# The block inverses of a gated delta rule: the two lower levels made in quadrants on the diagonal of the array

## Chip, cores and metric

The kernel runs on one core of one Trainium2 chip. The metric is the device time of one execution in microseconds (us). The time before is the median of three runs.

## What is computed

The reference is one transformer block over 1024 tokens: a projection, a gated delta rule with 8 heads, a sparse attention with 8 heads, and a gated merge of the two. The part that matters here is the delta rule. Per head and chunk of tokens a lower triangular system is solved:

```python
a_mat = where(strict, einsum('bhnid,bhnjd->bhnij', kb, k) * gamma, 0.0)
sol = triangular_solve(a_mat + eye, rhs, left_side=True, lower=True)
```

The kernel works with chunks of 128 tokens (the recurrence gives the same result for any chunk), so a head has `NT` = 8 systems of 128x128, and it makes the inverse of each rather than solving with it.

## The kernel before

The kernel has three phases: a front phase, the delta phase (`phase_delta`, line 1105) and attention with the merge. In the delta phase all engines walk through one list of slots, written out by hand. A head starts every 24 slots, and `u` is the slot counted from the head's start. In each slot TensorE first does a quarter of a projection (`project`, line 1805: six 16-bit matmuls of 128x512, by the helper `three`, lines 94 to 96), then the recurrence of up to two older heads (`recur`, lines 1937 to 1958, fp32 matmuls of 128x128), and in some slots a group of small fp32 matmuls of a head. The order on every engine is the order of the program; semaphores make one engine wait for another.

The inverse is built in levels. VectorE, ScalarE and GpSimd first make the inverses of the 16x16 diagonal blocks (`substitute` on GpSimd, `expand` on VectorE at u = 31). Then two neighbouring blocks of size b are joined, for b = 16, 32 and 64. The corner of the joined inverse is minus (lower block's inverse) x (corner of the system) x (upper block's inverse), so each level is two groups of matmuls with a step of another engine after each:

- b = 16: `middle16` (u 34, line 1886) multiplies the system `a_t` with `flip16`; VectorE masks the result out of PSUM into `x16` (u 35, line 1742); `outer16` (u 36, line 1892) multiplies `x16` with columns of `t2`; VectorE subtracts the result from `t2` (line 1726) and turns two 32x32 blocks per tile into `flip32` (line 1644).
- b = 32: `middle32` (u 38, line 1898); ScalarE copies PSUM to `x32` (line 1500); `outer32` (u 40, line 1904); VectorE subtracts two corners (line 1717) and turns three blocks into `flip64`.
- b = 64: `middle64` (u 42, line 1910), a copy (line 1496), `outer64` (u 44, line 1916), a subtraction (line 1709).

The groups of b = 16 and 32 use the full 128x128 array with 64 moving columns, since all blocks of a tile are handled in one matmul and mixed terms are zeroed by masks. The groups of b = 64 work on 64 rows and 64 columns of the array. Each group has 8 matmuls, one per tile. An fp32 matmul is two records in the trace, each with a weight load of its own. `middle` groups write PSUM bank 2, `outer` groups bank 3. `x16` and `x32` are the same memory, so VectorE zeroes the odd blocks again for each head (line 1737, u 46).

Of the kernel before, what the change touches and what calls it, by code (L numbers as in the profile page):

```python
# [25 lines left out]
P = 128  # L26
# [33 lines left out]
def constant_table():  # L60

    t = np.zeros((P, K_ALL), np.float32)
    i = np.arange(P)
    row, col = i[:, None], i[None, :]
    t[:, K_ID:K_ID + P] = row == col
    t[:, K_FLIP:K_FLIP + P] = row + col == P - 1
    t[:, K_UPTO:K_UPTO + P] = row <= col
    t[:, K_AFTER:K_AFTER + P] = row > col
    t[:, K_ONES:K_ONES + P] = 1.0
    t[:, K_CAUSAL:K_CAUSAL + P] = np.where(col > row, BELOW, 0)  # L70
    t[:, K_BLOCK:K_BLOCK + P] = row // 16 == col // 16

    short = np.arange(64)[None, :]
    t[:, K_PAIR:K_PAIR + 64] = row // 16 == 2 * (short // 16) + 1
    t[:, K_UNIT:K_UNIT + 16] = row % 16 == np.arange(16)[None, :]
    return t
# [1028 lines left out]
def phase_delta(nc, g, block):  # L1105

    with ExitStack() as ctx:
# [9 lines left out]
        prep = g.shared[:, 0:3 * T].rearrange("p (n t) -> p n t", t=T)  # L1117
        gam, x16 = (prep[:, n].rearrange("p (i n) -> p i n", n=P) for n in (0, 2))
        a_t = [part.rearrange("p (i n) -> p i n", n=P) for part in (prep[:, 1], g.arena[:, 10 * T:11 * T])]
# [9 lines left out]
        flip = lb[:, 0:NT * 32].rearrange("p (t two i) -> p t two i", two=2, i=32)  # L1129
        flip16 = lb[:, T // 2:T].rearrange("p (i n) -> p i n", n=64)  # L1130
        flip32, flip64 = (g.arena[:, (22 + n) * T // 2:(23 + n) * T // 2].rearrange("p (i n) -> p i n", n=64) for n in range(2))
        x32 = x16
        sq_junk, o_junk = sb("sq_junk", [P, 4, P], BF16), sb("o_junk", [P, P], BF16)
# [25 lines left out]
        at = lambda k, i: g.ps[:, k * BANK + i * P:k * BANK + (i + 1) * P]  # L1159
        half_at = lambda k, i: g.ps[:, k * BANK + i * 64:k * BANK + (i + 1) * 64]  # L1160
        win = g.w_in[0].rearrange("(k p) n -> p k n", p=P)
        wo = g.w_o_gdn[0].rearrange("(k p) n -> p k n", p=P)
# [208 lines left out]
        def _(act):  # L1371
# [108 lines left out]
            for slot in range(END):  # L1480
# [10 lines left out]
                for h in heads(slot):  # L1491
                    u = slot - SLOTS * h
                    if u == 42:
                        act.wait_ge(xm, 3 * h + 3)
                        act.wait_ge(tx, 3 * h + 2)
                        nc.scalar.copy(x32[64:128, :, 0:64], short(2)[64:128]).then_inc(x_ok, 1)
# [46 lines left out]
        def _(dve):  # L1543
            nc.vector.memset(raw[:, :, 0:PAD], 0.0).then_inc(pad, 1)
            nc.vector.memset(x16, 0.0).then_inc(pad, 1)
            nc.vector.memset(g.arena[:, 11 * T:12 * T], 0.0).then_inc(pad, 1)
            nc.vector.tensor_scalar(unseen, unseen, CLOSED, None, ALU.mult).then_inc(consts, 1)
# [76 lines left out]
            def expand(h):  # L1624
# [5 lines left out]
                for odd in range(2):  # L1630
# [5 lines left out]
                dve.wait_ge(turned, 2 * h + 2)  # L1636
                shape = [P, NT, 4, BASE]
                nc.vector.tensor_tensor(flip16.rearrange("p t (c i) -> p t c i", i=BASE),
                                        flip.rearrange("p t two i -> p (t two) i")[:, :, 0:BASE].unsqueeze(2).broadcast_to(shape),
                                        g.const[:, K_BLOCK:K_BLOCK + P].rearrange("p (c two i) -> p c two i", two=2, i=BASE)[:, :, 0].unsqueeze(1).broadcast_to(shape),  # L1640
                                        ALU.mult).then_inc(flip_ok, 1)

# [26 lines left out]
            for slot in range(END):  # L1669
# [7 lines left out]
                for h in heads(slot):  # L1677
# [34 lines left out]
                    if u == 40:  # L1712
                        dve.wait_ge(tx, 3 * h + 2)
                        for b in (0, 2):
                            odd, even = slice(32 * b + 32, 32 * b + 64), slice(32 * b, 32 * b + 32)
                            cols = slice(16 * b, 16 * b + 32)
                            nc.vector.tensor_tensor(t2[even, h % 3, :, odd], t2[even, h % 3, :, odd], short(3)[even, :, cols], ALU.subtract).then_inc(up, 1)
                        dve.wait_ge(up, 3 * h + 3)
# [5 lines left out]
                    if u == 36:  # L1724
                        dve.wait_ge(tx, 3 * h + 1)
                        nc.vector.tensor_tensor(blocks(t2[:, h % 3], 16, 1), blocks(t2[:, h % 3], 16, 1), short(3).rearrange("p i (c w) -> p i c w", w=16),
                                                ALU.subtract).then_inc(up, 1)
                        dve.wait_ge(up, 3 * h + 1)
# [3 lines left out]
                        flip_blocks(flip32, h, 0, 0, 0, 0)  # L1732
                        flip_blocks(flip32, h, 2, 2, 2, 1).then_inc(flip_ok, 1)
                    if u == 46:
                        dve.wait_ge(tx, 3 * h + 3)
                        dve.wait_ge(x_ok, 2 * h + 2)
                        nc.vector.memset(blocks(x16, 16, 1), 0.0).then_inc(pad, 1)
                    if u == 35:
                        dve.wait_ge(xm, 3 * h + 1)
                        dve.wait_ge(pad, 3 + h)  # L1740
                        shape = [P, NT, 4, 16]
# [60 lines left out]
        def _(pe):  # L1802
# [78 lines left out]
            def middle16(h):  # L1881
# [31 lines left out]
            def outer64(h):  # L1913
                pe.wait_ge(x_ok, 2 * h + 2)
                for i in range(NT):
                    last = mm(half_at(3, i)[0:64], x32[64:128, i, 0:64], t2[64:128, h % 3, i, 64:128], start=True, stop=True)
                last.then_inc(tx, 1)
# [711 lines left out]
```

## Time and profile before

| | us |
|---|---|
| median of 3 runs | 1448.59 (1444.6 to 1449.78) |
| the profiled execution | 1444.3 |
| its span, first to last instruction | 1442.2 |
| TensorE busy | 1402.8 (97%) |
| VectorE busy | 930.5 (65%) |
| ScalarE busy | 714.9 (50%) |
| GpSimd busy | 600.9 (42%) |
| mean granted TensorE clock | 0.995 |

TensorE's "busy" is the union of its matmuls' durations, and these overlap: a 128x512 matmul lasts 0.38 us and the next one starts 0.22 us after it. So costs on TensorE are read from the distance between starts in the timeline. PE is TensorE's matmuls, PEld its weight loads, DVE VectorE, ACT ScalarE, POOL GpSimd.

### The profile page before, as it was taken

Reading aid. Unit: us, or ns where it says so; the run is one execution under the profiler, and the core shown is the slowest. Engines: PE = TensorE matmul, PEld = TensorE weight load, DVE = VectorE, ACT = ScalarE, POOL = GpSimd, SP = SyncE. Lnnn points to the kernel's source line nnn. Section 1 sums busy time; section 2 is a strip of 40 time slices with the busy share of each in tenths; the row PEclk is TensorE's granted clock in tenths of the full one; section 3 lists DMA queues with packets and bytes.
Section 4 is the critical chain, followed back from the end, with each engine's and each line's share of the span. In section 5 each row is a group of like instructions: output and inputs, shape, how many; then the busy total and the mean of one; then the engine's idle time right before and its main releaser. Section 6 shows DMA issues by size and latency. Waiting matters only on the chain.

```text
span 1442.2 us, 26031 instructions
## 1 busy us (share of the span) xinstructions
PE 1402.8 (97%) x9792; PEld 872.8 (61%) x9792; DVE 930.5 (65%) x1946; ACT 714.9 (50%) x1513; POOL 600.9 (42%) x717
## 2 busy tenths in 40 slices
PE   6899999999999899999999999999999999999997
PEld 6546984444444567667667677655445888844444
DVE  3969777777335567678777775545724777737344
ACT  4848777785434544554555554333123777711111
POOL 0083677778652542541531521003022877764000
PEclk9999999999999999999999999999999999999999
DMA  9410343333224222231222322336663000075132
GB/s 373 122 37 2 105 118 118 117 106 117 88 80 130 73 61 71 63 90 45 76 61 62 89 61 74 103 103 222 198 217 141 28 19 31 16 266 175 36 107 88
DMA packets 137637, 147.43 MB, mean 102 GB/s; under 512 B 16706, under 2 KB 109738, under 8 KB 135852
## 3 DMA queue, kind: packets, MB, share of 16 engines
q1 hardware_dynamic: 136668, 141.31, 31.0%
q10 hardware_dynamic: 720, 4.46, 0.8%
q8 instruction: 77, 1.26, 0.4%
q14 instruction: 44, 0.36, 0.1%
q0 software_dynamic: 128, 0.03, 0.0%
HBM read 114.40 MB, written 31.15 MB: 101 GB/s over the span
## 4 chain that ended last, share of the span: by engine, by line
PE 61%; DVE 3%; ACT 2%; issue 1%; POOL 1%; DMA 0%; SPq 0%; DVEq 0%; ACTq 0%; POOLq 0%
PE ps L94 15%; PE ps L96 15%; PE ps L95 15%; PE ps L2368 2%; DVE g_yq L1562 1%; PE ps L1937 1%; PE ps L1892 1%; PE ps L1840 1%; PE ps L1904 1%; PE ps L1898 1%; DVE g_o L1697 1%; PE ps L1878 1%; PE ps L1958 1%; PE ps L1886 1%; PE ps L1942 1%
## 5 line engine op out<-in xcount | busy, mean ns | idle before, releaser
L94 PE MATMUL ps<-g_h_hi,g_piece_hi 128*128 128x512 f16 x544 | 206.7, 380 | 1.6 <-PEq L2579 1.6
L95 PE MATMUL ps<-g_h_lo,g_piece_hi 128*128 128x512 f16 x544 | 206.4, 379 | 0.0
L96 PE MATMUL ps<-g_h_hi,g_piece_lo 128*128 128x512 f16 x544 | 206.4, 379 | 0.0
L1328 POOL TENSOR_TENSOR g_shared<-g_shared 128x120 f32<-128x120 f32 (+14 forms) x120 | 56.5, 471 | 207.5 <-DMA g_shared<-diagonal_blocks 196.9
L946 DVE TENSOR_SCALAR_CACHE_REDUCE a_ada<-a_ada,a_s_all 128x896 bf16<-128x896 f32 (+1 forms) x124 | 113.1, 968 | 1.0
L94 PE MATMUL ps<-g_o,g_h_hi 128*128 128x128 f16 (+2 forms) x424 | 101.4, 266 | 1.7 <-DVE l_b L2489 1.6
L96 PE MATMUL ps<-g_o,g_h_lo 128*128 128x128 f16 (+2 forms) x424 | 101.4, 266 | 0.0
L95 PE MATMUL ps<-g_o,g_h_hi 128*128 128x128 f16 (+2 forms) x424 | 101.4, 266 | 0.0
L96 PEld LDWEIGHTS ps<-g_h_hi,g_piece_lo 128*128 128x128 bf16 x544 | 53.3, 98 | 64.4 <-issue 0.5
L1562 DVE SCALAR_TENSOR_TENSOR g_yq<-e_raw,g_taps,g_yq 128x1024 f32<-128x1024 f32 x60 | 86.5, 1442 | 8.8 <-ACT g_yq L1392 7.1
L94 PEld LDWEIGHTS ps<-g_h_hi,g_piece_hi 128*128 128x128 f16 x544 | 54.8, 101 | 53.4 <-issue 2.3
L95 PEld LDWEIGHTS ps<-g_h_lo,g_piece_hi 128*128 128x128 f16 x544 | 53.4, 98 | 51.2 <-issue 0.3
L2531 POOL TENSOR_SCALAR g_o<-g_o,l_share 128x128 f32<-128x128 f32 (+3 forms) x64 | 47.9, 749 | 80.0 <-DVE l_share L2474 79.6
L1553 DVE TENSOR_TENSOR g_piece_lo<-g_piece,g_piece_hi 128x1024 bf16<-128x1024 f32 x40 | 53.2, 1330 | 21.6 <-ACT g_piece_hi L1475 21.6
L1424 ACT ACTIVATE g_shared<-ps,e_s_neg 128x128 f32<-128x128 f32 x56 | 20.6, 367 | 93.5 <-PE ps L1942 93.2
L302 POOL TENSOR_TENSOR a_work<-a_w,a_work 128x512 bf16<-128x512 f32 x48 | 56.6, 1194 | 15.3 <-ACT a_work L683 15.3
L302 POOL TENSOR_TENSOR a_parts<-a_w,a_parts 128x512 bf16<-128x512 f32 x48 | 54.9, 1157 | 13.3 <-ACT a_parts L683 13.3
L2414 ACT ACTIVATE g_o<-g_o,l_top 128x128 f32<-128x128 f32 (+3 forms) x64 | 49.7, 776 | 20.7 <-DVE l_top L2467 18.7
L1330 POOL TENSOR_TENSOR g_shared<-g_shared 128x120 f32<-128x120 f32 (+14 forms) x120 | 54.1, 451 | 9.4
L700 ACT ACTIVATE a_ada<-a_ada,a_s_all 128x1024 bf16<-128x1024 f32 (+1 forms) x62 | 57.3, 927 | 0.5 <-DVEq L968 0.5
L1475 ACT CAST g_piece_hi<-g_piece 128x1024 f16<-128x1024 f32 x40 | 41.7, 1042 | 29.0 <-DMA g_piece<-in_w_o_gdn 28.0
L2423 ACT CAST g_o<-ps 128x128 f16<-128x128 f32 (+3 forms) x64 | 40.7, 637 | 26.5 <-PE ps L2368 24.9
(431 smaller groups left out, 4127.9 us busy)
## 6 DMA issues: line engine op xcount, KB each, us to landing
a_w<-in_w_in SPq DMA_DIRECT2D x17, 1024.0 KB, 5.7
g_piece<-in_w_in SPq DMA_DIRECT2D x34, 512.0 KB, 3.9
channel_gates<-a_ada SPq DMA_DIRECT2D x48, 256.0 KB, 2.2
g_shared<-diagonal_blocks SPq DMA_DIRECT2D x32, 256.0 KB
a_ada<-in_w_ada ACTq DMA_DIRECT2D x4, 1024.0 KB, 9.4
a_x<-in_x SPq DMA_DIRECT2D x8, 512.0 KB, 8.8
delta_gate<-a_ada SPq DMA_DIRECT2D x16, 256.0 KB, 2.5
g_shared<-sums_by_head SPq DMA_DIRECT2D x8, 512.0 KB, 3.9
```

Source lines behind the costliest of these rows:

```text
L94: pe.matmul(out, a_hi, b_hi, start=first, stop=False)
L95: pe.matmul(out, a_hi, b_lo, start=False, stop=False)
L96: return pe.matmul(out, a_lo, b_hi, start=False, stop=last)
L302: nc.gpsimd.tensor_tensor(op_lo[v % 2][:, x], of, op_hi[v % 2][:, x], ALU.subtract).then_inc(w_ready, 1)
L700: nc.scalar.activation(mask[:, g.first[i]:g.first[i + 1]], score[:, g.first[i]:g.first[i + 1]], ACT.Sign, bias=trial[:, 4 + e:5 + e], accu ...
L946: mark(("count", e), nc.vector.tensor_scalar(spent_of(i), rows_of(i), trial[:, e:e + 1], offset[:, e:e + 1], ALU.is_ge, ALU.add, accum_out ...
L1328: nc.gpsimd.tensor_tensor(part, table[:, j, :, j + 1:BASE], tc[:, :, j:j + 1].broadcast_to([P, NT, left]), ALU.mult).then_inc(sub, 1)
L1330: last = nc.gpsimd.tensor_tensor(tc[:, :, j + 1:BASE], tc[:, :, j + 1:BASE], part, ALU.subtract)
L1553: nc.vector.tensor_tensor(w_lo[:, m % 3], w32[:], w_hi[:, m % 3], ALU.subtract).then_inc(w_ready, 1)
L1562: nc.vector.scalar_tensor_tensor(out=y, in0=raw[:, m % 2, PAD - 3 + j:PAD - 3 + j + T], scalar=g.taps[:, tap:tap + 1], in1=y, op0=ALU.mult ...
L2414: nc.scalar.activation(p(n), p(n), ACT.Exp, scale=-1.0, bias=top[:, n % 4:n % 4 + 1], accum_out=total[:, n % 4:n % 4 + 1]).then_inc(exp_ok, 1)
L2531: nc.gpsimd.tensor_scalar(p(m), p(m), share[:, m % 4:m % 4 + 1], 1.0, ALU.mult, ALU.mult).then_inc(shared, 1)
```

## The change

The matmuls of b = 16 and b = 32 are split. For b = 16 the two 64x64 quadrants on the diagonal of the array are used, one matmul for each: 64 rows, 64 columns, 32 moving columns. For b = 32 a matmul uses 32 rows and 32 columns with 32 moving columns, in row groups 0 and 64 (`middle32`) or 32 and 96 (`outer32`). So each of the four groups has 16 matmuls in place of 8, alternating between the upper and the lower half. The upper half writes PSUM bank 2, the lower half bank 3, and `middle` and `outer` have separate halves of a bank. `flip16`, `flip32`, `x16` shrink to 32 columns per tile; `x32` and `x64` get memory of their own, so the zeroing of line 1737 goes. VectorE's mask and subtraction of b = 16 and ScalarE's copy of b = 32 become two instructions each, one per half. The b = 64 groups are unchanged but for where `x64` lies.

```diff
             def middle16(h):
...
                 for i in range(NT):
-                    last = mm(half_at(2, i), a_t[h % 2][:, i], flip16[:, i], start=True, stop=True)
+                    for half in range(HALVES):
+                        rows = quadrant(half)
+                        last = mm(edge(half, 0, i)[rows], a_t[h % 2][rows, i, rows], flip16[rows, i], start=True, stop=True)
             def outer16(h):
...
-                    last = mm(half_at(3, i), x16[:, i], columns(t2[:, h % 3, i], 16, 1), start=True, stop=True)
+                    for half in range(HALVES):
+                        rows = quadrant(half)
+                        last = mm(edge(half, 1, i)[rows], x16[rows, i], columns(t2[rows, h % 3, i, rows], 16, 1), start=True, stop=True)
             def middle32(h):
...
-                    last = mm(half_at(2, i), a_t[h % 2][:, i], flip32[:, i], start=True, stop=True)
+                    for half in range(HALVES):
+                        last = mm(edge(half, 0, i)[odd(half)], a_t[h % 2][even(half), i, odd(half)], flip32[even(half), i], start=True, stop=True)
             def outer32(h):
...
-                    last = mm(half_at(3, i), x32[:, i], columns(t2[:, h % 3, i], 32, 1), start=True, stop=True)
+                    for half in range(HALVES):
+                        last = mm(edge(half, 1, i)[even(half)], x32[odd(half), i], t2[odd(half), h % 3, i, odd(half)], start=True, stop=True)
...
+        edge = lambda half, part, i: g.ps[:, (2 + half) * BANK + part * 256 + i * 32:(2 + half) * BANK + part * 256 + (i + 1) * 32]
+        edges = lambda half, part, rows: g.ps[rows, (2 + half) * BANK + part * 256:(2 + half) * BANK + (part + 1) * 256].rearrange("p (i n) -> p i n", n=32)
+        quadrant = lambda half: slice(64 * half, 64 * half + 64)
...
                     if u == 38:
...
-                        nc.scalar.copy(blocks(x32, 32, 0), short(2).rearrange("p i (c w) -> p i c w", w=32)).then_inc(x_ok, 1)
+                        nc.scalar.copy(x32[odd(0)], edges(0, 0, odd(0)))
+                        nc.scalar.copy(x32[odd(1)], edges(1, 0, odd(1))).then_inc(x_ok, 1)
...
                     if u == 36:
...
-                        nc.vector.tensor_tensor(blocks(t2[:, h % 3], 16, 1), blocks(t2[:, h % 3], 16, 1), short(3).rearrange("p i (c w) -> p i c w", w=16),
-                                                ALU.subtract).then_inc(up, 1)
+                        for half in range(HALVES):
+                            rows = quadrant(half)
+                            corners = blocks(t2[rows, h % 3, :, rows], 16, 1)
+                            last = nc.vector.tensor_tensor(corners, corners, edges(half, 1, rows).rearrange("p i (c w) -> p i c w", w=16), ALU.subtract)
+                        last.then_inc(up, 1)
...
-                    if u == 46:
...
-                        nc.vector.memset(blocks(x16, 16, 1), 0.0).then_inc(pad, 1)
                     if u == 35:
...
-                        nc.vector.tensor_tensor(blocks(x16, 16, 0), short(2).rearrange("p i (c w) -> p i c w", w=16),
-                                                g.const[:, K_PAIR:K_PAIR + 64].rearrange("p (c w) -> p c w", w=16).unsqueeze(1).broadcast_to(shape),
-                                                ALU.mult).then_inc(x16_ok, 1)
+                        for half in range(HALVES):
+                            rows = quadrant(half)
+                            last = nc.vector.tensor_tensor(blocks(x16[rows], 16, 0), edges(half, 0, rows).rearrange("p i (c w) -> p i c w", w=16),
+                                                           lower[rows].unsqueeze(1).broadcast_to([64, NT, 2, 16]), ALU.mult)
+                        last.then_inc(x16_ok, 1)
```

## Rows read from the trace of the kernel before

**Rows 1.** The page, 40 slices: PE busy tenths, granted clock tenths

```profile
PE   6899999999999899999999999999999999999997
...
PEclk9999999999999999999999999999999999999999
```

**Rows 2.** Stretches of the delta phase: us, busy us (instructions) by engine, clock

```profile
480.00:530.00 50.00, 45.32 (x276) 30.34 (x275) 31.22 (x59) 19.15 (x38) 19.57 (x35) 0.93 0.22 61
530.00:880.00 350.00, 346.69 (x2315) 240.02 (x2315) 263.56 (x572) 188.53 (x472) 129.38 (x218) 1.00 0.24 68
```

**Rows 3.** Waits of TensorE from 530 to 880 us: total, times, longest

```profile
PE ps L1937 <- DVE g_o L1666: 2.6, 2, 1.4
```

**Rows 4.** Line 1892: durations in ns, forms, how many records

```profile
L1892 PE MATMUL ps<-g_arena,g_shared x128: 222/275/422, 499.4 to 891.7; 128*128 128x64 f32 x128
```

**Rows 5.** Timeline of TensorE, head 1: start us, length us, what, xcount

```profile
547.54 1.90 PE L1886 MATMUL ps<-g_shared,g_arena 128*128 128x64 f32 x16
549.27 0.38 PE L94 MATMUL ps<-g_h_hi,g_piece_hi 128*128 128x512 f16 x1
...
552.31 1.90 PE L1892 MATMUL ps<-g_arena,g_shared 128*128 128x64 f32 x16
...
558.69 1.90 PE L1898 MATMUL ps<-g_arena 128*128 128x64 f32 x16
...
563.46 1.90 PE L1904 MATMUL ps<-g_arena,g_shared 128*128 128x64 f32 x16
```

**Rows 6.** The same timeline at the groups on a quadrant of 64x64

```profile
568.23 1.04 PE L1851 MATMUL ps<-g_const,g_shared 128*128 128x128 f32 x8
569.20 1.14 PE L1910 MATMUL ps<-g_arena 64*64 64x64 f32 x16
570.27 0.39 PE L94 MATMUL ps<-g_h_hi,g_piece_hi 128*128 128x512 f16 x1
```

**Rows 7.** Front phase: six matmuls on two row groups of 64 rows, and their forms

```profile
103.57 0.82 PE L480 MATMUL ps<-a_ada 64*128 64x512 f16 x6 [0.24 <-DVE a_ada L1051]
```

**Rows 8.** Forms and durations (ns) of those six, from 103.5 to 104.1 us

```profile
L480 PE MATMUL ps<-a_ada x6: 323/354/387, 103.6 to 104.0; 64*128 64x512 f16 x3, 64*128 64x384 f16 x3
```

**Rows 9.** Front phase timeline: small fp32 matmuls with 24 rows and 24 moving columns

```profile
90.54 0.42 PE L454 MATMUL ps<-g_const,a_ada 24*128 24x24 f32 x4
```

**Rows 10.** Attention phase timeline: first and last of 27 matmuls in a row

```profile
1151.94 0.22 PE L94 MATMUL ps<-g_o,g_h_hi 128*128 128x128 f16 x1
...
1153.39 0.22 PE L96 MATMUL ps<-g_arena 128*128 128x128 f16 x1
```

**Rows 11.** Other engines by line and form: total us, mean ns, idle before

```profile
L1638 DVE TENSOR_TENSOR g_shared<-g_shared,g_const 128x512 f32<-128x512 f32 x8 | 9.8, 1219 | 0.0
L1717 DVE TENSOR_TENSOR g_arena<-g_arena,ps 32x256 f32<-32x256 f32 x16 | 6.6, 414 | 12.3 <-PE ps L1904 12.0
L1742 DVE TENSOR_TENSOR g_shared<-ps,g_const 128x512 f32<-128x512 f32 x8 | 5.4, 678 | 1.8 <-PE ps L1886 1.8
L2221 DVE TENSOR_TENSOR g_arena<-g_arena 128x256 f32<-128x256 f32 x2 | 0.8, 425 | 0.1
L1737 DVE MEMSET g_shared<- 128x512 f32 x8 | 3.9, 485 | 0.4
L1500 ACT COPY g_shared<-ps 128x512 f32<-128x512 f32 x8 | 4.7, 586 | 38.7 <-PE ps L1898 38.7
L2423 ACT CAST g_o<-ps 128x256 f16<-128x256 f32 x8 | 3.0, 370 | 1.4 <-PE ps L2368 1.3
```

**Rows 12.** Timeline of VectorE and ScalarE between the groups of head 1

```profile
550.59 0.68 DVE L1742 TENSOR_TENSOR g_shared<-ps,g_const 128x512 f32<-128x512 f32 x1
554.97 0.88 DVE L1644 STREAM_TRANSPOSE g_arena<-g_arena 32x256 f32<-32x256 f32 x2
560.63 0.59 ACT L1500 COPY g_shared<-ps 128x512 f32<-128x512 f32 x1 [4.20 <-PE ps L1898]
```

More of the change, by code:

```diff
@@ L73, in constant_table @@
     short = np.arange(64)[None, :]
-    t[:, K_PAIR:K_PAIR + 64] = row // 16 == 2 * (short // 16) + 1
+    t[:, K_PAIR:K_PAIR + 64] = row // 16 % 4 == 2 * (short // 16 % 2) + 1 - short // 32
     t[:, K_UNIT:K_UNIT + 16] = row % 16 == np.arange(16)[None, :]
@@ L1117, in phase_delta @@
         prep = g.shared[:, 0:3 * T].rearrange("p (n t) -> p n t", t=T)
[L1118 removed]
+        gam = prep[:, 0].rearrange("p (i n) -> p i n", n=P)
+        x16, x32 = (prep[:, 2, c0:c0 + NT * n].rearrange("p (i n) -> p i n", n=n) for c0, n in ((0, 64), (NT * 64, 32)))
         a_t = [part.rearrange("p (i n) -> p i n", n=P) for part in (prep[:, 1], g.arena[:, 10 * T:11 * T])]
@@ L1129, in phase_delta @@
         flip = lb[:, 0:NT * 32].rearrange("p (t two i) -> p t two i", two=2, i=32)
-        flip16 = lb[:, T // 2:T].rearrange("p (i n) -> p i n", n=64)
-        flip32, flip64 = (g.arena[:, (22 + n) * T // 2:(23 + n) * T // 2].rearrange("p (i n) -> p i n", n=64) for n in range(2))
-        x32 = x16
+        flip16 = lb[:, T // 2:3 * T // 4].rearrange("p (i n) -> p i n", n=32)
+        flip32 = g.arena[:, 11 * T:11 * T + NT * 32].rearrange("p (i n) -> p i n", n=32)
+        flip64, x64 = (g.arena[rows, 23 * T // 2:12 * T].rearrange("p (i n) -> p i n", n=64) for rows in (slice(0, 64), slice(64, P)))
+        lower, upper = (g.const[:, c0:c0 + 32].rearrange("p (c w) -> p c w", w=BASE) for c0 in (K_PAIR, K_PAIR + 32))
         sq_junk, o_junk = sb("sq_junk", [P, 4, P], BF16), sb("o_junk", [P, P], BF16)
@@ L1160, in phase_delta @@
         half_at = lambda k, i: g.ps[:, k * BANK + i * 64:k * BANK + (i + 1) * 64]
+        edge = lambda half, part, i: g.ps[:, (2 + half) * BANK + part * 256 + i * 32:(2 + half) * BANK + part * 256 + (i + 1) * 32]
+        edges = lambda half, part, rows: g.ps[rows, (2 + half) * BANK + part * 256:(2 + half) * BANK + (part + 1) * 256].rearrange("p (i n) -> p i n", n=32)
+        quadrant = lambda half: slice(64 * half, 64 * half + 64)
+        even, odd = (lambda half, e=e: slice(64 * half + 32 * e, 64 * half + 32 * e + 32) for e in range(2))
         win = g.w_in[0].rearrange("(k p) n -> p k n", p=P)
@@ L1495, in _ @@
                         act.wait_ge(tx, 3 * h + 2)
-                        nc.scalar.copy(x32[64:128, :, 0:64], short(2)[64:128]).then_inc(x_ok, 1)
+                        nc.scalar.copy(x64, short(2)[64:128]).then_inc(x_ok, 1)
                     if u == 38:
@@ L1636, in expand @@
                 dve.wait_ge(turned, 2 * h + 2)
-                shape = [P, NT, 4, BASE]
+                shape = [P, NT, 2, BASE]
                 nc.vector.tensor_tensor(flip16.rearrange("p t (c i) -> p t c i", i=BASE),
                                         flip.rearrange("p t two i -> p (t two) i")[:, :, 0:BASE].unsqueeze(2).broadcast_to(shape),
-                                        g.const[:, K_BLOCK:K_BLOCK + P].rearrange("p (c two i) -> p c two i", two=2, i=BASE)[:, :, 0].unsqueeze(1).broadcast_to(shape),
-                                        ALU.mult).then_inc(flip_ok, 1)
+                                        upper.unsqueeze(1).broadcast_to(shape), ALU.mult).then_inc(flip_ok, 1)
             def flip_blocks(out, h, rows, cols, to_rows, to_cols):
@@ L1713, in _ @@
                         dve.wait_ge(tx, 3 * h + 2)
[L1714 to L1717, printed above, removed]
+                        for half in range(HALVES):
+                            corner = t2[even(half), h % 3, :, odd(half)]
+                            nc.vector.tensor_tensor(corner, corner, edges(half, 1, even(half)), ALU.subtract).then_inc(up, 1)
                         dve.wait_ge(up, 3 * h + 3)
@@ L1903, in outer32 @@
                 for i in range(NT):
-                    last = mm(half_at(3, i), x32[:, i], columns(t2[:, h % 3, i], 32, 1), start=True, stop=True)
+                    for half in range(HALVES):
+                        last = mm(edge(half, 1, i)[even(half)], x32[odd(half), i], t2[odd(half), h % 3, i, odd(half)], start=True, stop=True)
                 last.then_inc(tx, 1)
@@ L1915, in outer64 @@
                 for i in range(NT):
-                    last = mm(half_at(3, i)[0:64], x32[64:128, i, 0:64], t2[64:128, h % 3, i, 64:128], start=True, stop=True)
+                    last = mm(half_at(3, i)[0:64], x64[:, i], t2[64:128, h % 3, i, 64:128], start=True, stop=True)
                 last.then_inc(tx, 1)
```

9 lines of the change are left out of this document (3 added, 6 removed).

## The prediction, made before the changed kernel was run

> **What bounds the kernel now.** I read first the page's slices. TensorE stands at nine tenths or more in nearly every slice and its clock is granted in full [rows 1], so it is never slowed by idling and every later price is read at the 2.4 GHz level. "Busy" on TensorE can hide slack, so next come the stretches and the waits. From 530 to 880 us, six of the eight heads, TensorE is busy 346.7 of 350.0 us; VectorE is second with 263.6, that is 75% [rows 2]. The largest wait of TensorE in that stretch is 2.6 us in all [rows 3], against 350. So in the delta phase TensorE's instruction stream is the bound: a microsecond taken off it should shorten the kernel by nearly one, until something that TensorE waits for is late. The first head, 480 to 530, is looser (45.3 of 50) [rows 2].
>
> **How the groups are paid now.** A group is paid by the distance from its first start to the next group's first start. `middle16` starts at 547.54 and the following matmul at 549.27: 1.73 us [rows 5]. Line 1892 has 128 records, and 8 heads x 8 matmuls x 2 records are 128 [rows 4]; lines 1886, 1898 and 1904 have the same shape and the same length of 1.90 us [rows 5]. The step between two records is (1.90 - 0.275)/15 = 108 ns, with 0.275 the duration of one [rows 4, 5]. That is as much as a step of line 1851, with 128 moving columns where this has 64: 0.97/8 is at most 121 ns [rows 6]. So moving columns don't set it; the weights' 128 columns do. Cutting the weights' columns is therefore the lever, and the change cuts them to 64 and to 32, at twice the number of records (32 per group).
>
> **The price of a 64x64 record** stands in the trace: line 1910 starts at 569.20 and the next matmul at 570.27, 1.07 us for 16 [rows 6]. It has 64 moving columns where the new ones have 32, so this is an upper bound for one quadrant. Entering costs something as well: eight records of line 1851 at (1.04 - 0.275)/7 = 0.109 each are 0.87, but the distance to line 1910 is 0.97 [rows 6], so 0.10 us more. The new groups at b = 16 lie, like the old, between full-array matmuls, so each enters and leaves once: 1.07 + 0.10 = 1.17 us for one quadrant's 16 records.
>
> **The disputed term: do the two quadrants run at the same time?** If yes, a b = 16 group costs about 1.17 (both quadrants lie beside each other). If no, the second quadrant's 16 records come behind the first: (1.14 - 0.22)/15 = 61 ns each, so 1.17 + 16 x 0.061 = 2.15 us, which is above the 1.73 of now. The nearest rows for overlap are six matmuls on two row groups of 64 rows in the front phase: three of 512 and three of 384 columns [rows 8] took 0.82 us in all [rows 7]. One after the other they would need at least 3 x 0.216 + 2 x 0.162 + 0.32 = 1.29 us (0.216 is the step of 512 columns, 0.162 that scaled to 384, 0.32 the last one's duration [rows 8]). So matmuls of different row groups did run beside each other, and each went to another bank, as the two halves do in the change. What these rows don't show is the same for fp32 weights, or for groups of columns. I take overlap.
>
> **b = 16**: 1.73 - 1.17 = 0.56 us saved per group, 16 groups (2 x 8 heads): 9.0 us. From the other side: 1.73 - 2.15, 6.7 us lost.
>
> **b = 32**: weights of 32x32. No row has this form. From 128 to 64 weight columns the step fell from 108 to 61 ns, 0.73 ns a column; 32 columns further down it would be 61 - 24 = 37 ns, and 16 records in a quadrant save another 16 x 0.024 = 0.38 us: 0.79 for a group. The other end is that nothing goes below some 60 ns: the smallest fp32 matmuls in the trace, 24 rows and 24 moving columns, took 0.42 us for four, (0.42 - 0.215)/3 = 68 ns a step [rows 9], though their weights had 128 columns. Then a group costs 1.17 as at b = 16. I take 0.90, nearer the first, since the step fell with the columns in the rows of the same kind: 1.73 - 0.90 = 0.83 us, 16 groups: 13.3 us. Ends with overlap: 9.0 and 15.0; without it: 0.79 + 16 x 0.037 = 1.38, 5.6 saved, or 2.15, 6.7 lost.
>
> The Trainium skill, "TensorEngine Tiling (Array Packing)", section Instruction Overhead, says a matmul carries about 60 cycles of overhead and that one should not tile a dimension that is small already. An estimate from that page: 32 records x 25 ns = 0.8 us, with entering and leaving about 1.05 for b = 32, which would make the sum 2.4 us smaller. No run so far shows records of different quadrants at that density; the sum above doesn't use it.
>
> **VectorE.** Mask and subtraction at b = 16: one instruction of 128x512 at 0.68 us becomes two of 64 rows and 256 elements; 256 elements from PSUM took 0.41 [rows 11], so +0.15 each, twice. `flip16`'s product halves: 1.22 us mean for 512 elements, 0.43 for an addition of 256 in the same memory [rows 11], so -0.6 to -0.8. The zeroing, 0.49, goes [rows 11]. Sum per head -0.8 us, of some 42: a head's period is (891.7 - 1.7 - 499.4)/7 = 56 us [rows 4], and 75% of it is 42. ScalarE's copy of 0.59 becomes two of about 0.37 [rows 11]: +0.15. None of this is on TensorE's stream; it decides only whether TensorE finds its inputs.
>
> **What is late next.** Head 1: the mask ends at 551.27 and `outer16` starts at 552.31, 1.0 us later; the turned blocks are ready at 555.85 for `middle32` at 558.69, 2.8 us; ScalarE's copy ends at 561.22 for `outer32` at 563.46, 2.2 us [rows 5, 12]. Between two groups lie the projections and recurrence of two slots, 552.31 - 549.27 = 3.0 us [rows 5], that stay. With `middle16` shorter the mask can still only start when VectorE is free, so of the 1.0 us about 1.0 - 0.56 - 0.15 = 0.3 is left. So the groups don't yet stall each other, but the four groups lie within 17 us and gain 2.8 us there, and the recurrence behind them waits on VectorE too. VectorE would be at 41 of 53 us per head, 78%. I charge 10% of the gain for such waits: what queues behind a late group is the next projection, so it is paid in full.
>
> **Sum.** 9.0 + 13.3 = 22.3 us; less 10% is 20 us. The profiled execution took 1444.3 us, 2.1 above its span; that would be 1424. It lies 4.3 below the median of the three runs, 1448.59, and since I forecast a median I apply the 20 us there: 1428.5 us. Likeliest case's own range: 13 us (waits eat 30%, b = 32 at 1.17) to 28 us (b = 32 at 0.79, no waits, a few us from VectorE's relief): 1420 to 1436.
>
> **Rivals.**
>
> 1. *The quadrants go one after the other, each at its columns' price.* Then b = 16 loses 6.7 and b = 32 wins 5.6: 1 us slower, 1450. For it: no fp32 row shows overlap, and the two records of one fp32 matmul follow each other on the same quadrant, so the order is AABB and the hardware must look two records ahead. Against: rows 7. Chance 0.10.
>
> 2. *Every record costs some 60 ns, whatever its size and quadrant* (an issue price). 32 records instead of 16: each group 2.15, 32 groups x 0.42 = 13 us slower: 1462. It decides once a record costs on average more than (1.73 - 0.10 - 0.15)/31 = 48 ns, where 0.15 is the distance at leaving, 1.07 less 15 steps of 0.061. For it: no fp32 step in the trace is under 60 ns. Against: 16-bit matmuls of attention go at (1153.39 - 1151.94)/26 = 56 ns [rows 10], which is about what their 128 columns need, and the six of rows 7 came closer together. The Trainium skill, "TensorE: Matmul & The Clock Gate", section Back-to-back issue gap, knows such a price, about 62 ns per matmul when the sequencer decodes in software; an estimate from it is 32 x 62 ns = 2.0 us a group, the same outcome. Chance 0.09.
>
> 3. *Overlap as forecast, but VectorE's order takes the gain back*: the mask and the turned blocks come late, TensorE waits at `outer16` and at line 1937, and only half of the 22 us arrives: 1438. For it: VectorE at 75% with little slack at `outer16`. Against: the stretches between groups, 3.0 us for two slots, are already shorter than any slot pair with a group will be, and TensorE doesn't wait in them. Chance 0.13.
>
> Forecast 0.68. What a measurement of this kernel can tell from no change is about 0.5%, 7 us. Faster by over 0.5%: forecast and most of rival 3, and a little of rival 1 if b = 32 does better: 0.78. Within 0.5%: 0.13. Slower: rival 2: 0.09. The range for 8 in 10 is 1418 to 1446: below, the best of all terms; above, rival 3 and the better half of rival 1.
>
> **What would show it.** The group of `middle16`: 32 records within 1.1 to 1.2 us, start to next start, and single starts of the lower half only a few ns from the upper half's. If the group lasts about 2.1, overlap is wrong; if b = 16 lasts 1.2 and b = 32 the same, the columns' price has a floor. TensorE's waits from 530 to 880 us should grow from 3 us to no more than some 5; if they grow by over 8, rival 3 is right. The period of a head should go from 56 to about 53.5 us. My forecast is wrong if the time is above 1436 or below 1420.

## The result, and the profile after

| | before | after |
|---|---|---|
| median, us | 1448.72 (4 runs) | 1423.54 (1422.03 to 1429.42, 4 runs) |
| ratio, 95% interval | | 0.9838 (0.9806 to 0.9869) |
| span of the profiled execution, us | 1442.2 | 1419.9 |
| TensorE busy, us | 1402.8 | 1375.4 |
| VectorE busy, us | 930.5 | 926.2 |
| waits of TensorE from 480 to 930 us | 7.9 | 11.0 |
| first record of `middle16` to last of `outer64`, starts, us | 490.9 to 912.3 | 491.0 to 888.5 |

The kernel is 25 us faster at the median, 22.3 in the profiled executions. Forecast were 20 us and 1428.5, likeliest 1420 to 1436, range 1418 to 1446.

First the groups of head 1 in the timeline of TensorE in the changed kernel (start us, length us, line, shapes, xcount, idle before), to be set beside rows 5:

```profile
539.46 0.39 PE L1953 MATMUL ps<-g_shared,g_yq 128*128 128x128 f32 x2
539.78 1.12 PE L1893 MATMUL ps<-g_shared,g_arena 64*64 64x32 f32 x32
540.83 0.39 PE L94 MATMUL ps<-g_h_hi,g_piece_hi 128*128 128x512 f16 x1
...
546.36 1.12 PE L1901 MATMUL ps<-g_arena,g_shared 64*64 64x32 f32 x32 [2.32 <-DVE g_shared L1747]
...
553.52 0.38 PE L1948 MATMUL ps<-g_shared,g_yq 128*128 128x128 f32 x2
553.84 0.69 PE L1908 MATMUL ps<-g_arena 32*32 32x32 f32 x32
554.47 0.39 PE L94 MATMUL ps<-g_h_hi,g_piece_hi 128*128 128x512 f16 x1
```

`middle16` (now line 1893) takes 540.83 - 539.78 = 1.05 us with 32 records, where it took 1.73 with 16 [rows 5]. That is the footprint of 16 records of 64x64 on one quadrant [rows 6], so the second quadrant's 16 cost nothing: in the trace a record of one half starts 6 to 7 ns after one of the other, and the next pair mostly 51 to 52 ns later. `middle32` (line 1908) takes 554.47 - 553.84 = 0.63 us. Both are entered 0.10 us late: two records of line 1953 are 0.22 us, and the distance is 539.78 - 539.46 = 0.32. In all eight heads the 32 groups have these lengths within 4 ns, where no wait falls into them.

The waits of TensorE from 480 to 930 us, in the kernel before and then in the changed one (who waits, for whom, total us, times, longest); the line left out of the first is that of rows 3:

```profile
PE ps L1892 <- DVE g_shared L1742: 4.0, 1, 4.0
...
PE ps L1886 <- DVE g_shared L1638: 0.7, 1, 0.7
PE ps L1937 <- DVE g_o L1663: 0.6, 3, 0.2
```

```profile
PE ps L1901 <- DVE g_shared L1747: 5.1, 2, 2.8
PE ps L1948 <- DVE g_o L1672: 3.3, 3, 1.4
PE ps L1948 <- DVE g_o L1669: 1.7, 3, 0.7
PE ps L1893 <- DVE g_shared L1645: 0.9, 1, 0.9
```

The stream became 16 x (1.73 - 1.05 - 0.10) = 9.3 us shorter at b = 16 and 16 x (1.73 - 0.63 - 0.10) = 16.0 at b = 32, 25.3 in all. Against it stand 11.0 - 7.9 = 3.1 us more of waits in the delta phase. The new one is the one with the thinnest slack of rows 5 and 12: `outer16` of head 1 waits 2.3 us for the mask, which lies behind a convolution in VectorE's order. The others are the recurrence. One more wait, which the kernel before doesn't have, comes at 1028 us, behind the heads (view from 930 us on):

```profile
PE ps L2019 <- DVE g_arena L1793: 1.6, 1, 1.6
```

The last term is TensorE's clock. In the kernel before it fell after the 4.0 us wait of the first head. In the changed one it stayed at 1.00 there, in spite of a wait of 2.8 us, and fell after the 2.3 us wait in head 1. First a stretch of the kernel before, then two of the changed one (the number behind the last bracket is the granted clock), and line 1845 with 16 records in head 0 and in head 1 of the changed kernel:

```profile
500.00:510.00 10.00, 10.00 (x51) 8.05 (x51) 6.54 (x30) 4.21 (x5) 0.00 (x0) 0.66 0.02 3
```

```profile
540.00:550.00 10.00, 7.68 (x94) 6.09 (x91) 9.21 (x18) 4.92 (x8) 5.60 (x3) 0.89 0.02 5
550.00:560.00 10.00, 10.00 (x107) 5.81 (x107) 8.23 (x31) 3.81 (x10) 0.00 (x0) 0.94 0.23 56
```

```profile
498.64 2.05 PE L1845 MATMUL ps<-g_yq 128*128 128x128 f32 x16
...
547.41 3.41 PE L1845 MATMUL ps<-g_yq 128*128 128x128 f32 x16
```

In head 1 the 16 records lie mostly at the 1.2 GHz level, in head 0 at 2.4. The lower clock cost about 10 x 0.34 = 3.4 us before and 10 x (0.11 + 0.06) = 1.7 us after, so 1.7 us were given back. With it the books of these two executions close: 25.3 - 3.1 - 1.6 + 1.7 = 22.3 us, and the span became 22.3 shorter. The stretch of the heads (last row of the table) became 23.9 shorter, which is 25.3 - 3.1 + 1.7. Waits and clock differ between executions, though. Two more profiled executions of the changed kernel (the repeats below) have 7.9 and 9.4 us of waits from 480 to 930 us, and 2.9 and 1.2 us at line 2019. So only the 25.3 us of the stream is the same in all; new waits take 2.7 to 4.7 us of it.

VectorE and ScalarE in the changed kernel, by line and form (total us, mean ns, idle before):

```profile
L1645 DVE TENSOR_TENSOR g_shared<-g_shared,g_const 128x256 f32<-128x256 f32 x8 | 11.5, 1436 | 0.0
L1734 DVE TENSOR_TENSOR g_arena<-g_arena,ps 64x256 f32<-64x256 f32 x16 | 6.7, 418 | 6.4 <-PE ps L1901 6.3
L1747 DVE TENSOR_TENSOR g_shared<-ps,g_const 64x256 f32<-64x256 f32 x16 | 6.7, 416 | 1.3 <-PE ps L1893 1.2
L1506 ACT COPY g_shared<-ps 32x256 f32<-32x256 f32 x8 | 2.9, 362 | 21.0 <-PE ps L1908 21.0
```

The halves cost what rows 11 said: 0.42 us each on VectorE, 0.36 on ScalarE. `flip16`'s product (line 1645) has a mean of 1.44 us with half the elements, where it was 1.22 [rows 11], but both means mix two cases. In four heads it took 0.41 us, where the same product took 0.68 in six heads of the kernel before. In the other four it took 2.13 to 2.57 us, and each time an instruction of 128x1024 was running on GpSimd (line 1348 or 1344) and VectorE's product ended 0.3 us after it:

```profile
536.87 0.42 DVE L1645 TENSOR_TENSOR g_shared<-g_shared,g_const 128x256 f32<-128x256 f32 x1
...
641.53 3.21 POOL L1348 TENSOR_TENSOR g_shared<-g_shared,g_const 128x1024 f32<-128x1024 f32 x1
...
642.45 2.56 DVE L1645 TENSOR_TENSOR g_shared<-g_shared,g_const 128x256 f32<-128x256 f32 x1
```

In the kernel before that met two heads, with 2.84 us. So half the elements save 0.27 us, and the product met GpSimd's instruction in two heads more.

### The profile page after: what moved, and what is told of

Its sections match the earlier page's. It is cut to its first block, busy times and chain, and to the rows that moved or that the text cites. A ratio compares the mean times of both kernels' runs of the same rounds, so it can differ in the third digit from the quotient of the medians.

```text
span 1419.9 us, 27055 instructions
## 1 busy us (share of the span) xinstructions
PE 1375.4 (97%) x10296; PEld 840.6 (59%) x10304; DVE 926.2 (65%) x1954; ACT 716.5 (50%) x1521; POOL 596.5 (42%) x717
## 4 chain that ended last, share of the span: by engine, by line
PE 53%; DVE 6%; DMA 3%; issue 2%; ACT 2%; POOL 2%; SPq 1%; DVEq 0%; POOLq 0%; ACTq 0%
PE ps L94 14%; PE ps L96 14%; PE ps L95 13%; DVE g_yq L1569 2%; PE ps L2379 2%; DMA merge_half<-g_shared 1%; DVE g_o L1703 1%; POOL g_shared L1334 1%; PE ps L1948 1%; PE ps L1845 1%; POOL g_shared L1336 1%; PE ps L1969 1%; PE ps L1953 1%; PE ps L1952 1%; PE ps L1968 1%
## 5 line engine op out<-in xcount | busy, mean ns | idle before, releaser
L94 PE MATMUL ps<-g_o,g_h_hi 128*128 128x128 f16 (+2 forms) x424 | 101.4, 266 | 1.7 <-DVE l_b L2500 1.6
L95 PE MATMUL ps<-g_o,g_h_hi 128*128 128x128 f16 (+2 forms) x416 | 98.3, 264 | 0.0
L1560 DVE TENSOR_TENSOR g_piece_lo<-g_piece,g_piece_hi 128x1024 bf16<-128x1024 f32 x40 | 50.0, 1250 | 22.8 <-ACT g_piece_hi L1481 22.8
L302 POOL TENSOR_TENSOR a_parts<-a_w,a_parts 128x512 bf16<-128x512 f32 x48 | 55.0, 1161 | 13.3 <-ACT a_parts L683 13.3
```

Of the source, the lines that this page charges most:

```text
L94: pe.matmul(out, a_hi, b_hi, start=first, stop=False)
L95: pe.matmul(out, a_hi, b_lo, start=False, stop=False)
L302: nc.gpsimd.tensor_tensor(op_lo[v % 2][:, x], of, op_hi[v % 2][:, x], ALU.subtract).then_inc(w_ready, 1)
L1560: nc.vector.tensor_tensor(w_lo[:, m % 3], w32[:], w_hi[:, m % 3], ALU.subtract).then_inc(w_ready, 1)
```

## The experiments

Each kernel below is an edit of the changed kernel. Times are medians; "group" is the distance from a group's first start to the next matmul, without the 0.10 us for entering. The runs came in three sets, each with its own runs of the kernel before: 1449.69 (first four), 1448.4 (next four), 1450.54 us (last three). The ratio and its interval are computed from the single runs of both kernels and are not the quotient of the two medians.

| run | median us | ratio to before (95%) | group b = 16 | group b = 32 |
|---|---|---|---|---|
| only b = 32 | 1435.07 | 0.9888 (0.9838 to 0.9938) | 1.73 | 0.63 |
| halves outermost | 1442.4 | 0.9946 (0.9923 to 0.997) | 1.77 | 1.03 |
| same rows | 1422.89 | 0.9802 (0.975 to 0.9854) | 1.05 | 0.63 |
| same columns | 1424.73 | 0.9812 (0.9756 to 0.9868) | 1.05 | 0.63 |
| same tile | 1446.05 | 0.9986 (0.9959 to 1.0012) | 1.98 | 1.13 |
| one bank | 1425.56 | 0.9866 (0.9822 to 0.9909) | 1.05 | 0.63 |
| four tiles | 1422.26 | 0.9844 (0.9789 to 0.99) | 0.66 | 0.63 |
| changed kernel again | 1425.5 | 0.9854 (0.9807 to 0.99) | 1.05 | 0.63 |
| runs of four | 1431.91 | 0.9876 (0.9856 to 0.9897) | 1.36 | 0.83 |
| four tiles, one set of columns | 1418.03 | 0.9777 (0.9748 to 0.9805) | 0.66 | 0.63 |
| changed kernel, third time | 1425.24 | 0.9834 (0.9813 to 0.9854) | 1.05 | 0.63 |

**One part alone.** The b = 16 groups, mask and subtraction go back to full width:

```diff
-                    for half in range(HALVES):
-                        rows = quadrant(half)
-                        last = mm(edge(half, 0, i)[rows], a_t[h % 2][rows, i, rows], flip16[rows, i], start=True, stop=True)
+                    last = mm(half_at(2, i), a_t[h % 2][:, i], flip16[:, i], start=True, stop=True)
```

> Only the b = 32 groups stay in 32x32 tiles; the b = 16 groups go back to the full array with 64 moving columns (x32 keeps memory of its own, so the zeroing stays away). In the changed kernel a b = 16 group took 1.05 us from its start to the next group's start and 0.09 more to enter, a b = 32 group 0.63 and 0.09, against 1.73 before. Theory (TensorE's stream is the bound and each group pays its own footprint): 16 groups x (1.73 - 1.15) = 9.4 us are given back, less a part of the some 3 us that waits took: 1431 to 1433. Rival (the gain is in VectorE's relief, -0.8 us per head, and in waits, not in the footprints): nearly the whole gain of 25 us stays, about 1425.

Measured 1435.1, in its profile the groups at 1.73 and 0.63. Against the changed kernel's 1423.5 to 1425.5 that gives back 10 to 12 us where the footprints say 9.4, and lies 2 us above the 1431 to 1433 expected. In the profiled executions the stretch from the first record of `middle16` to the last of `outer64` is 404.3 us where the changed kernel's is 397.5, so 6.8 us are given back, with 3.0 us less of waits. So the gain follows the footprints of the groups, and the larger share, some 14.6 us against before in the same set, is b = 32's.

**The halves one after the other.**

```diff
-                for i in range(NT):
-                    for half in range(HALVES):
+                for half in range(HALVES):
+                    for i in range(NT):
```

> The changed kernel with the two loops of the four groups exchanged: first the eight tiles of the upper half (16 records), then the eight of the lower half. The same matmuls, banks and operands. Theory A (each row group has a queue of its own and TensorE takes what is behind in the order when its row group is free): records of the two halves still start side by side, groups last 1.05 and 0.63 as before, 1423.5. Theory B (overlap needs the two halves next to each other in the order, TensorE looks only few records ahead): the second half runs behind the first, 16 x 58 ns = 0.93 us more at b = 16 and 16 x 32 ns = 0.5 us more at b = 32, 16 groups of each: 23 us more on the stream, about 1446.

In the timeline of this kernel, groups of one head:

```profile
651.36 1.84 PE L1893 MATMUL ps<-g_shared,g_arena 64*64 64x32 f32 x32
653.13 0.39 PE L94 MATMUL ps<-g_h_hi,g_piece_hi 128*128 128x512 f16 x1
...
663.73 1.09 PE L1908 MATMUL ps<-g_arena 32*32 32x32 f32 x32
664.75 0.39 PE L94 MATMUL ps<-g_h_hi,g_piece_hi 128*128 128x512 f16 x1
```

The same 32 records take 1.77 us instead of 1.05, and the median rises by 17 to 19 us (its own profiled execution was its fastest, 1434.0, at a mean granted clock of 0.997 where the others had 0.988 to 0.993). The footprints alone give 16 x (1.77 - 1.05) + 16 x (1.03 - 0.63) = 17.9 us. Theory B holds in the main: overlap wants neighbours in the order. But its 23 us were too many, since not all is serial: 1.98 would be (same tile, below), so some 0.2 us overlap where one half meets the other.

**Which difference allows the overlap?** Two kernels take away one difference each, the third both. The lower half's matmuls read the upper half's rows, or write to its place, or both. So none of the three makes the lower blocks of the inverse; number and shapes of the instructions stay. Of each diff the line of `middle16` is shown; the other groups are edited alike.

```diff
 # same rows
+                        last = mm(edge(half, 0, i)[rows], a_t[h % 2][quadrant(0), i, rows], flip16[quadrant(0), i], start=True, stop=True)
 # same columns
+                        last = mm(edge(half, 0, i)[quadrant(0)], a_t[h % 2][rows, i, rows], flip16[rows, i], start=True, stop=True)
 # same tile
+                        last = mm(edge(half, 0, i)[quadrant(0)], a_t[h % 2][quadrant(0), i, quadrant(0)], flip16[quadrant(0), i], start=True, stop=True)
```

> The lower half's matmuls read the upper half's rows (the array's rows 0 to 63, or 0 to 31 and 32 to 63), but still write the lower half's partitions, so both halves use one row group and different column groups. The inverse's lower blocks are then wrong in value; the number and shapes of all instructions are those of the changed kernel. Theory (row groups are what runs side by side): the halves follow each other, groups of 1.98 and 1.13 us, 23 us more than the changed kernel, about 1446. Rival (column groups of their own are enough): 1.05 and 0.63, 1423.5.

> The lower half's matmuls keep their rows but write the upper half's partitions (in their own bank), so the two halves use different row groups and one column group. The lower blocks of the inverse are then wrong in value. Theory (different row groups and different banks are enough, as for the front phase's 64-row matmuls, which have all 128 columns): groups of 1.05 and 0.63 us, 1423.5. Rival (the diagonal is needed, both kinds of group must differ): 1.98 and 1.13, about 1446.

> Both halves' matmuls of the four groups read the upper half's rows and write the upper half's partitions, alternating only between bank 2 and bank 3, so all 32 records of a group are on one tile of the array. The lower blocks of the inverse are wrong in value; instructions, shapes and order are those of the changed kernel. The runs before showed 1.05 and 0.63 us per group with only the rows or only the columns different, and 1.77 and 1.03 with the halves one after the other; in all of these an alternation of tiles went with an alternation of banks. Theory (two different tiles of the array are what runs side by side): now nothing overlaps, 107 + 30 x 58 + 151 ns = 2.0 us at b = 16 and 0.63 + 16 x 0.032 = 1.13 us at b = 32, 23 us more on the stream than the changed kernel, about 1445. Rival (alternating banks is what matters): 1.05 and 0.63, 1423.5.

`middle16` of one head in each, first same rows, then same columns, then same tile:

```profile
645.83 1.12 PE L1893 MATMUL ps<-g_shared,g_arena 64*64 64x32 f32 x32
646.89 0.39 PE L94 MATMUL ps<-g_h_hi,g_piece_hi 128*128 128x512 f16 x1
```

```profile
648.97 1.12 PE L1893 MATMUL ps<-g_shared,g_arena 64*64 64x32 f32 x32
650.02 0.39 PE L94 MATMUL ps<-g_h_hi,g_piece_hi 128*128 128x512 f16 x1
```

```profile
658.21 2.05 PE L1893 MATMUL ps<-g_shared,g_arena 64*64 64x32 f32 x32
660.19 0.39 PE L94 MATMUL ps<-g_h_hi,g_piece_hi 128*128 128x512 f16 x1
```

The theory of "same rows" fell: with one row group and two column groups the overlap is as full as on the diagonal. "Same columns" went as its theory said. Only when both are the same is it gone, and then each record costs (2.05 - 0.22)/31 = 59 ns at b = 16, with 0.22 its duration. In these runs the condition is two different tiles of the array, in rows or in columns; the diagonal isn't needed. "Same tile" also excludes that alternating banks does it: there the banks still alternate. It is the no-overlap case of the prediction, run. With its groups at 1.98 and 1.13 and the entering, the stream is 16 x (1.73 - 1.13 - 0.10) - 16 x (1.98 + 0.10 - 1.73) = 2.4 us shorter than before, and 1446.05 beside 1448.4 is 2.4 us faster. Rival 1 of the prediction had that case at 1 us slower.

**The banks.**

```diff
-        edge = lambda half, part, i: g.ps[:, (2 + half) * BANK + part * 256 + i * 32:(2 + half) * BANK + part * 256 + (i + 1) * 32]
+        edge = lambda half, part, i: g.ps[:, (2 + part) * BANK + half * 256 + i * 32:(2 + part) * BANK + half * 256 + (i + 1) * 32]
```

> The changed kernel with both halves in the same bank: the middle groups write bank 2 (upper half's results in columns 0 to 255, lower half's in 256 to 511), the outer groups bank 3. Rows and columns of the array as changed. Theory (different tiles are enough): groups of 1.05 and 0.63 us, 1423.5. Rival (two tiles can't write one bank at the same time): the records alternate without overlap, 2.0 and 1.13 us, about 1445, and should two writes collide, the output is wrong.

```profile
649.54 1.12 PE L1893 MATMUL ps<-g_shared,g_arena 64*64 64x32 f32 x32
650.59 0.39 PE L94 MATMUL ps<-g_h_hi,g_piece_hi 128*128 128x512 f16 x1
```

The same 1.05 us and, set beside the changed kernel on the same chip, the same time (1425.56 and 1425.5). The halves don't need a bank of their own for the overlap; that part of the change buys nothing here. The Trainium skill, "TensorEngine Tiling (Array Packing)", section Gotcha 1: PSUM Pressure, says that different row tiles can't access one bank at the same time. The trace doesn't bear this out for tiles that write different partitions: 1.05 us a group with one bank and with two. Tiles that write the same partitions were run only with two banks.

**Four tiles.** Each group of b = 16 in four tiles of 32x32:

```diff
+                    for q in range(4):
+                        c, rows = q % 2, slice(32 * q, 32 * q + 32)
+                        last = mm(edge(q // 2, 0, i)[rows, 16 * c:16 * c + 16], a_t[h % 2][rows, i, rows], flip16[rows, i, 16 * c:16 * c + 16], start=True, stop=True)
```

> The b = 16 groups in four tiles of 32x32 with 16 moving columns in place of two of 64x64 with 32 (64 records a group in place of 32; tiles 0 and 1 in bank 2, tiles 2 and 3 in bank 3); mask and subtraction become four instructions of 32 rows and 128 elements each. b = 32 as in the changed kernel. Theory (each tile pays 32 ns per record for its own 16 records and four tiles run side by side): 0.63 us a group in place of 1.05, 16 groups save 6.8 us, less some waits for VectorE, which has some 0.5 us more per head: 1418 to 1421. Rival 1 (records can't start closer than the 16 ns on average that b = 32 showed): 64 x 16 = 1.0 us plus 0.1 to leave, 1.15 us a group, 1.5 us slower than changed. Rival 2 (TensorE looks too few matmuls ahead to keep four tiles going, or a shared bank serializes two of them): 1.1 us or more, 1424 to 1432.

> The changed kernel itself, on the same chip as the other three, so that they can be compared with it: 1423.5, groups of 1.05 and 0.63 us.

```profile
649.83 0.73 PE L1893 MATMUL ps<-g_shared,g_arena 32*32 32x16 f32 x64
650.49 0.39 PE L94 MATMUL ps<-g_h_hi,g_piece_hi 128*128 128x512 f16 x1
```

64 records in 0.66 us, 10 ns apiece. Rival 1's floor of 16 ns doesn't exist, nor does rival 2's. The stream is 16 x 0.39 = 6.3 us shorter, but the median is only some 3 us lower (1422.26 against 1425.5, with intervals that overlap), and above the 1418 to 1421 expected. So the footprint is shown by the trace, the gain in time is not shown. The trace has where part of it went: TensorE waits 4.9 us for the mask, now four instructions, in four heads, where the changed kernel beside it waits 2.8 us in one.

**How far ahead?** Four tiles of one half, then four of the other, twice:

```diff
-                for i in range(NT):
-                    for half in range(HALVES):
+                for half, i in [(half, i) for first in (0, 4) for half in range(HALVES) for i in range(first, first + 4)]:
```

> The changed kernel's groups in the order: four tiles of the upper half, four of the lower, four upper, four lower. With eight at a time (halves outermost) only the last two matmuls of the first half and the first two of the second overlapped, 1.77 and 1.03 us a group. Theory (TensorE looks two matmuls ahead, an fp32 matmul being two records): each of the three changes of half overlaps two matmuls and saves four steps: 1.98 - 3 x 4 x 0.058 = 1.28 us at b = 16, 1.126 - 3 x 4 x 0.032 = 0.74 to 0.83 us at b = 32; 16 x (0.23 + 0.15) = 6 us slower than the changed kernel, 1430 to 1432. Rival (it looks four or more ahead when the queue is full): 1.05 and 0.63, as changed.

Groups of 1.36 and 0.83 us, 1431.9 against 1425.2 for the changed kernel beside it: 6.7 us slower, in the range of the theory, though its group at b = 16 was to be 1.28. Each of the three changes of half saves (1.98 - 1.36)/3 = 0.21 us, 3.5 steps of 59 ns where the theory had four, so almost two matmuls of two records each. The one change of "halves outermost" saves the same 1.98 - 1.77 = 0.21. At b = 32 it is (1.13 - 0.83)/3 = 0.10 us, 3.1 steps of 32 ns.

**A version from what the runs showed.** Four tiles at b = 16, all writing the same 16 columns per tile of one bank on their own partitions, so that the mask is one instruction for all of them:

```diff
+        edge16 = lambda part, i: g.ps[:, (2 + part) * BANK + i * BASE:(2 + part) * BANK + (i + 1) * BASE]
...
+                        last = mm(edge16(0, i)[rows], a_t[h % 2][rows, i, rows], flip16[rows, i], start=True, stop=True)
...
+                        nc.vector.tensor_tensor(x16[:, :, 0:BASE], edges16(0), lower, ALU.mult).then_inc(x16_ok, 1)
```

> Four tiles of 32x32 at b = 16 as in the run before (0.66 us a group), and, since two tiles wrote one bank side by side, all four write the same 16 columns per tile of one bank, each its own 32 partitions. So the mask is one instruction of 128x128 instead of two of 64x256 (0.28 for 0.83 us), flip16's product is half as large, ScalarE's copy of b = 32 is one instruction again; the subtraction at b = 16 takes four instructions of 32x128 (some 1.1 for 0.83). Per head VectorE has 0.4 us less than in the changed kernel. Theory (TensorE's stream is still the bound, waits for the mask go): 16 x 0.39 = 6.3 us off the stream and 2 to 3 us of waits: 1416 to 1418 where the changed kernel is at 1424 to 1425. Rival 1 (the recurrence waits for VectorE take the gain): 1421 or more. Rival 2 (four tiles writing the same bank and columns get in each other's way): groups above 0.66 us, 1424.

> The changed kernel itself beside the other two, on the same chip: 1423 to 1426.

1418.03 us, 7.2 less than the changed kernel beside it (1425.24), and the intervals of the two against before don't touch. A group, the mask, and the waits of TensorE from 480 to 930 us in it:

```profile
647.88 0.73 PE L1887 MATMUL ps<-g_shared,g_arena 32*32 32x16 f32 x64
648.54 0.39 PE L94 MATMUL ps<-g_h_hi,g_piece_hi 128*128 128x512 f16 x1
```

```profile
L1743 DVE TENSOR_TENSOR g_shared<-ps,g_const 128x128 f32<-128x128 f32 x8 | 2.2, 276 | 0.8 <-PE ps L1887 0.8
```

```profile
PE ps L1942 <- DVE g_o L1670: 3.9, 4, 1.5
PE ps L1895 <- DVE g_shared L1743: 2.6, 1, 2.6
PE ps L1942 <- DVE g_o L1667: 1.9, 3, 0.7
...
```

The group is 0.66 as forecast, so four tiles don't disturb each other in one bank and on the same columns. The time is 0.03 us above the end of the 1416 to 1418 expected, and 7.2 us is about the 6.3 us of the stream. The 2 to 3 us of waits that were expected on top didn't go: here they are 9.2 us in all (2.6 for the mask, 5.8 for the recurrence, 0.8 for others), in the changed kernel beside it 9.4 (3.6 for the mask, 5.5 for the recurrence, 0.3 for another).

## Why the prediction was right, step by step

- *TensorE's stream is the bound, and a group is paid by its footprint.* Right, and shown: footprints, waits and clock give the 22.3 us of the profiled executions, and "only b = 32" moved by its groups.
- *The clock is granted in full, TensorE never slowed by idling.* Not quite: the prediction's own row for 480 to 530 us has 0.93 [rows 2], about 3.4 us lost after a wait of 4.0. It priced no clock, and 1.7 us of the gain came from there in this pair of executions. That is luck.
- *The weights' columns set the step, not the moving ones.* Half shown. The moving columns don't: on one tile of 64x64 a step is 58 ns with 64 of them (line 1910) and 58 to 59 with 32 ("same tile"). But rows and columns of the weights shrink together in every group here: steps of 112 ns at 128x128, 58 at 64x64, 32 at 32x32 (1.13 us for 32 records on one tile). Against columns alone stand the records of rows 9, with 24 rows and 128 columns: 68 ns on average, not 112. Which of the two sets the step stays open. That nothing goes below some 60 ns (the upper end, from rows 9) is refuted.
- *Entering and leaving, 0.10 us and the rest in the 1.07 of line 1910.* Right to 0.02.
- *Overlap.* Right in the outcome, too narrow in the reason. I argued from rows 7 for different row groups in different banks. Same rows with different columns overlap as well, and one bank does. Of the signs, the starts of the two halves are 6 to 7 ns apart as forecast; the 1.1 to 1.2 us for `middle16`, start to next start, came out as 1.05, since the 0.10 for entering lies before its first start.
- *b = 16 saves 9.0.* Measured 9.3.
- *b = 32 saves 13.3.* This was the mis-sized term: 16.0. I took 0.90 us for a group between 0.79 and 1.17, and it was 0.63 + 0.10 = 0.73, below both ends. The steps of 108 and 61 ns were averages that took in an odd first step: in line 1886 the second record starts 58 ns after the first and every other one 111 to 112 after the last, in line 1910 the second starts 107 ns after the first and every other one 58 to 59. From 112 and 58 the same working gives 31 ns at 32 columns and 0.74 us for the group. The prediction's side estimate of 25 ns a record, 0.8 us for 32, was too high as well: 0.63 us, and 0.66 for 64 records on four tiles.
- *Ten per cent lost to waits, 2.3 us.* Too little: 4.7 us in this execution, 2.9 and 2.7 in the repeats. Of the 4.7, 2.9 were at the places named, `outer16` and the recurrence; that VectorE would also be late behind the heads (line 2019, 1.2 to 2.9 us) was not foreseen. The sign for the waits from 530 to 880 us, no more than some 5, was missed too: 7.3 us, and 4.9 and 6.3 in the repeats. The period of a head went from 56 to 53.0 us, by the prediction's own working; 53.5 was forecast.
- *VectorE 0.8 us less per head.* Wrong: the instructions that the change edits cost 0.3 us more over all eight heads (mask 6.7 for 5.4, subtraction 6.7 for 5.5, `flip16`'s product 11.5 for 9.8, and 3.9 for the zeroing gone). The estimate for `flip16` started from the mean of 1.22, which two long ones had raised. VectorE's busy time fell by 4.3 us all the same, most of it in a subtraction that the change doesn't touch (line 1560, 50.0 us where it was 53.2).
- *The sum.* 1.7 us too little for the clock and 3.0 for the footprints, 2.4 too much for the waits: 22.3 where 20 was forecast. The medians lie 25.2 us apart (22.9 and 25.3 for the repeats beside their own runs of the kernel before); what is beyond 22.3 is the spread between executions.
- *The rivals.* Serial quadrants (1) is what "same tile" ran; it would have cost nearly the whole gain. An issue price (2) is refuted by 10 ns a record. Waits taking half (3) didn't happen: 11 to 19%.

## What to carry to other kernels

Where a stream of small fp32 matmuls binds, look at the size of the weights, not at the moving columns (up to the 128 seen here): cutting the weights to the block that is needed and putting independent blocks on different tiles of the array made a group of eight matmuls 2.6 times shorter (1.73 to 0.66 us; 2.3 times with the 0.10 for entering). Interleave the tiles matmul by matmul; with each half in one block the same instructions lose 17 to 19 of the 25 us. Look at what the shorter stream then meets: waits of TensorE took 11 to 19% of it here. Lay the tiles' results on the same columns of one bank, each on its own partitions, and what reads them can stay one instruction.

## What the runs showed of the hardware that was not expected

- Two tiles that share their rows, or their columns, run side by side as fully as two on the diagonal; 59 ns a record on one tile became 29 ((1.12 - 0.22)/31) with two.
- Two tiles running side by side and writing one bank cost nothing (1.05 us a group either way), and four writing even the same columns of it on other partitions neither (0.66).
- TensorE behaves as if it reached about two fp32 matmuls ahead, not further: "halves outermost" and "runs of four" both save 3.5 steps per change of half at b = 16, and 3.1 at b = 32. That is inferred from the lengths of the groups.
- Records on four tiles started 10 ns apart on average, over 64 of them.
- A VectorE product of 0.41 us took 2.13 to 2.57 us when it started beside a running instruction of 128x1024 on GpSimd, and ended 0.3 us after that.
- Executions of one kernel go with the mean granted clock: the last version took 1414.3 us at 0.996 and 1424.4 at 0.985. Part of that arises in the front phase, which no edit here touches. From 90 to 130 us the clock was granted in full in one execution of the changed kernel, less in its first repeat, and still less in "only b = 32", in this order:

```profile
90.00:130.00 40.00, 37.82 (x225) 17.75 (x224) 38.41 (x57) 33.01 (x60) 28.17 (x30) 1.00 0.10 30
```

```profile
90.00:130.00 40.00, 39.17 (x204) 18.33 (x204) 35.35 (x52) 29.74 (x55) 28.13 (x30) 0.83 0.10 30
```

```profile
90.00:130.00 40.00, 38.39 (x163) 17.58 (x162) 29.44 (x44) 23.58 (x43) 28.12 (x30) 0.66 0.10 30
```

  Their first `middle16` started at 491.0, 493.8 and 500.7 us. Why the clock fell in one execution and not in another isn't shown; TensorE was busy 37.8 to 39.2 of these 40 us in all three.
